# Experts' rows in 32-row units, up to four experts to a block, and inputs laid out by the host

## The chip, the core and the metric

The program runs on one core of a Trainium2 chip. TensorE (PE) multiplies, VectorE (DVE) and ScalarE (ACT) work on the results, GpSimd (POOL) issues the indirect transfers and SyncE (SP) most of the others. All numbers are fp32. The metric is the device time of one execution in microseconds (us); lower is better.

## What is computed

Two blocks of a network over 1024 tokens (and 256 context tokens), D = 1024 columns. The first has two layers, each with a modulation by a vector, a projection `h @ w_in`, latent attention, two convolution branches and an output projection. The second has three mixers (SSD, RWKV, GLA) and then a mixture of experts, the part that the change is mostly about:

```python
def _moe_ffn(h, router_w, router_b, w1, w3, w2, sw1, sw3, sw2):
    ...
    scores = jax.nn.sigmoid((h @ router_w).astype(f32))
    sel = scores + router_b.astype(f32)
    grp_score = lax.top_k(sel.reshape(t, N_GROUPS, per_group), 2)[0].sum(-1)
    _, top_g = lax.top_k(grp_score, TOPK_GROUPS)
    ...
    _, idx = lax.top_k(sel, TOP_K)
    wts = jnp.take_along_axis(scores, idx, axis=1)
    wts = wts / jnp.sum(wts, -1, keepdims=True) * ROUTED_SCALE
    ...
    def body(acc, blk):
        tok, wt, e = blk
        xb = h[tok]
        hid = jax.nn.silu(xb @ w1[e]) * (xb @ w3[e])
        return acc.at[tok].add(wt[:, None] * (hid @ w2[e]).astype(f32)), None
    ...
    shared = (jax.nn.silu(h @ sw1) * (h @ sw3)) @ sw2
    return routed.astype(h.dtype) + shared
```

Each of 1024 tokens goes to 8 of 64 experts, 8192 rows in all. An expert has w1 and w3 of 1024x256 and w2 of 256x1024, 3 MB together. The reference's own routing of these inputs gives the experts from 29 to 315 rows each.

## The kernel before

The kernel is one hand-ordered program: each stage is a set of functions, one for each engine, and an engine runs its instructions in the order in which they were emitted. Generators joined by `staged((n, lane), ...)` take turns, lane by lane, from step n on. Between stages `gate()` makes SP wait for everything and then lets all engines go on.

**Start.** `vectors()` (line 330) loads the constants and 34 small vectors as rows, turns them into columns on PE (line 348) and copies them out on DVE. `beginning()` then reads `x` and `ctx` in ten tiles of 128 tokens (`tokens`, line 456): SP loads a tile (line 470), PE turns it with eight 128x128 transposes (line 481), DVE copies it to `X` (line 489). Between the tiles run the modulation, whose matmuls (line 416) have two stationary columns and put four 512-column blocks of the weights into PSUM partitions 0, 32, 64 and 96, and the sums of squares of the norms (line 545, `n0` to `n2` for the token blocks of 256, 512 and 512). A norm ends with DVE lines 590 to 597 and ACT line 632, and then the projection (line 754) starts. `second_to_third` reads the two tiles of `ctx_2` in the same way.

**Routing** (`route_*` in `moe_sparse`, line 2680). After the choice of experts, PE counts each expert's rows (line 2767), DVE turns counts into blocks of 128 rows (lines 2851 to 2872), PE ranks the rows within each expert (lines 2770, 2773), and DVE works out a slot for each of the 8192 rows (`slots_of`). POOL writes token number and weight of each into the list `l_d` with 64 indirect DMAs (line 2947); SP then loads the list as `LB`, one column of 128 rows per block. Rows that no token has point at a dummy row.

**Expert blocks** (`blocks`, line 3046). NS = 96 blocks are always run and up to 127 where the counts want it (`rest`). The counts of these inputs fill 94. A block is 128 rows of one expert. SP loads the expert's three matrices into one of six slots (line 3072, three DMAs of 1 MB, only where a block is the first of its expert). POOL gathers the 128 rows of `h_d` (line 3082) three blocks ahead. For block q, in this order, PE does `up(q)`: eight matmuls with the turned rows as stationary operand and 512 columns of w1 and w3 moving (line 3128); `turn_h(q-1)`: two transposes (line 3136); `turn_x(q+1)`: eight transposes (line 3111); `down(q-1)`: four matmuls of 512 columns (line 3147). DVE and ACT empty PSUM after each (lines 3173 to 3220), and POOL adds the block's result to `r_d` by an indirect DMA (line 3090), which waits until the block before has landed. Each fp32 matmul is two instructions in the trace, so line 3128 has 16 for a block and line 3147 eight.

**End.** Eight tiles of 128 tokens are normalised and stored.

## Time and profile before

| | us |
|---|---|
| median of 3 runs | 5219.56 |
| lowest, highest | 5213.47, 5234.58 |
| the profiled execution | 5191.66 |
| its span, first to last instruction | 5189.8 |
| PE busy in it | 4463.7 (86%) |
| expert blocks, first matmul of line 3128 to last of line 3147 | 3996.57 to 5096.62 |
| DVE, ACT and POOL busy in the span | 2030.3, 1389.0, 516.4 |

The profile is one execution. Its rows name engine, line and operation, and what ended the idle time before them. A matmul's printed duration holds its way through the array, so neighbours overlap: the distance from one row's start to the next row's is the cost, not the sum of the durations.

### The profile page before, as it was taken

The page shows a single profiled execution, that of the slowest core. Times are in us where ns is not written, and L with a number is a line of the kernel's source. Part 1 is how long each engine was busy: PE and PEld are TensorE (multiplying, and loading weights), DVE is VectorE, ACT ScalarE, POOL GpSimd, SP SyncE. Part 2 cuts the span into 40 slices and gives each one's busy share as a digit, 9 for nine tenths or more (in the row PEclk, how much of TensorE's full clock was granted, in tenths as well). Part 3 has the DMA queues.
Part 4 walks back from the last instruction along what each step waited for, and adds up shares of the span by engine and source line. Part 5 has one row for each costly group of instructions (what it writes and reads, how often), then busy time and mean ns, then how long its engine had stood idle before and what let it go on. Part 6 is the DMA issues. An engine that isn't in the chain of part 4 may idle for free. (4 is left out here: it accounts for less than half of the span.)

```text
span 5189.8 us, 68095 instructions
## 1 busy us (share of the span) xinstructions
PE 4463.7 (86%) x25844; PEld 2575.7 (50%) x25844; DVE 2030.3 (39%) x4201; ACT 1389.0 (27%) x3178; POOL 516.4 (10%) x552
## 2 busy tenths in 40 slices
PE   5999799999987999999977437885977999999992
PEld 3454466644444664445466326773444444444441
DVE  2641556523416662320055576665252111111115
ACT  2111545411126551211133423331031111111110
POOL 0000000000000000000000002221005222222220
PEclk8999889999998999999977659886978999999996
DMA  4011000210110004302110110002015789899974
GB/s 179 18 60 60 13 13 17 91 63 28 58 59 5 13 15 189 114 30 72 62 44 2 60 36 3 3 3 71 36 56 193 215 245 320 276 283 317 305 236 126
DMA packets 290595, 517.79 MB, mean 100 GB/s; under 512 B 24853, under 2 KB 202847, under 8 KB 285023
## 3 DMA queue, kind: packets, MB, share of 16 engines
q1 hardware_dynamic: 249582, 377.69, 21.2%
q0 software_dynamic: 40688, 135.67, 9.3%
q8 instruction: 217, 3.56, 0.3%
q14 instruction: 108, 0.88, 0.1%
HBM read 511.88 MB, written 102.09 MB: 118 GB/s over the span
## 5 line engine op out<-in xcount | busy, mean ns | idle before, releaser
L754 PE MATMUL banks<-arena 128*128 128x512 f32 (+1 forms) x2928 | 1108.0, 540 | 15.4 <-DMA arena<-in_w_in 9.7
L754 PEld LDWEIGHTS banks<-arena 128*128 128x128 f32 x2928 | 558.9, 191 | 562.8 <-issue 522.7
L3128 PE MATMUL banks<-arena 128*128 x1536 | 678.0, 594 | 13.6 <-DMA arena<-in_exp_w 12.5
L3128 PEld LDWEIGHTS banks<-arena 128*128 128x128 f32 x1536 | 292.8, 191 | 382.5 <-issue 382.5
L941 PE MATMUL banks<-arena 128*128 128x512 f32 (+1 forms) x896 | 373.2, 571 | 25.2 <-DMA arena<-y_d 17.7
L1305 PE MATMUL banks<-arena 96*128 96x512 f32 (+1 forms) x800 | 377.0, 555 | 11.7 <-ACT arena L1408 10.0
L3147 PE MATMUL banks<-arena 128*128 x768 | 346.1, 593 | 1.4 <-ACT arena L3207 1.4
L1355 DVE TENSOR_REDUCE arena<-banks 128x1 f32<-128x512 f32 (+1 forms) x400 | 238.1, 595 | 243.2 <-PE banks L1305 241.6
L3186 DVE SCALAR_TENSOR_TENSOR arena<-arena,banks 128x256 f32<-128x256 f32 x96 | 46.2, 482 | 650.0 <-ACT arena L3220 650.0
L941 PEld LDWEIGHTS banks<-arena 128*128 128x128 f32 x896 | 171.9, 193 | 218.3 <-issue 212.5
L1313 PEld LDWEIGHTS banks<-arena 128*128 128x128 f32 x1312 | 171.9, 143 | 154.2 <-issue 123.5
L1408 ACT ACTIVATE arena<-banks,arena 128x512 f32<-128x512 f32 (+1 forms) x400 | 239.3, 606 | 16.1 <-DVE arena L1364 2.8
L3090 POOL DMA_INDIRECT r_d<-arena x96 | 151.7, 1580 | 824.0 <-DVE arena L3179 790.4
L1313 PE MATMUL banks<-arena 128*128 128x128 f32 x1312 | 214.0, 277 | 0.1
L1414 ACT ACTIVATE arena<-banks 128x256 f32<-128x256 f32 (+1 forms) x272 | 131.6, 484 | 289.4 <-PE banks L1313 289.2
L3147 PEld LDWEIGHTS banks<-arena 128*128 128x128 f32 x768 | 138.0, 189 | 139.7 <-issue 139.7
L1326 PE MATMUL banks<-arena 128*64 128x128 f32 x2624 | 191.9, 283 | 17.2 <-DVE arena L1369 13.1
L3220 ACT ACTIVATE arena<-banks 128x256 f32<-128x256 f32 x96 | 37.1, 387 | 618.8 <-PE banks L3128 618.8
L953 DVE SCALAR_TENSOR_TENSOR arena<-banks,arena 128x512 f32<-128x512 f32 (+1 forms) x56 | 39.9, 712 | 385.4 <-PE banks L941 385.4
L772 ACT ACTIVATE arena<-banks 128x512 f32<-128x512 f32 (+1 forms) x94 | 51.4, 547 | 514.1 <-PE banks L754 514.0
L780 ACT ACTIVATE arena<-banks 128x512 f32<-128x512 f32 (+3 forms) x95 | 50.5, 532 | 464.9 <-PE banks L754 459.5
L861 DVE SCALAR_TENSOR_TENSOR arena<-arena 128x1296 f32<-128x1296 f32 (+1 forms) x120 | 171.2, 1427 | 4.3
(500 smaller groups left out, 5859.2 us busy)
## 6 DMA issues: line engine op xcount, KB each, us to landing
arena<-in_exp_w SPq DMA_DIRECT2D x288, 1024.0 KB, 16.1
arena<-in_ada_w SPq DMA_DIRECT2D x12, 2048.0 KB, 7.4
arena<-in_w_in SPq DMA_DIRECT2D x19, 1024.0 KB, 5.7
arena<-in_w_mod SPq DMA_DIRECT2D x8, 2048.0 KB
arena<-in_w_in SPq DMA_DIRECT2D x7, 2048.0 KB
arena<-in_w_out SPq DMA_DIRECT2D x6, 2048.0 KB
arena<-in_w_mod SPq DMA_DIRECT2D x8, 1024.0 KB
u<-arena POOLq DMA_DIRECT2D x28, 256.0 KB, 2.3
```

Source lines behind the costliest of these rows:

```text
L754: i = e.matmul(self.out_of(n), lhs, rhs, start=k == 0, stop=k == KT - 1)
L861: e.scalar_tensor_tensor(z[:, lo:hi], a[:, lo - 15 + j:hi - 15 + j], reg(cw + 2 * j + ft, 1), z[:, lo:hi], ALU.mult, ALU.add).then_inc(Vn. ...
L941: i = e.matmul(bank(n % 4)[:, 0:nn], w[:, q, :], H[:, q, t0:t0 + nn], start=q == 0, stop=q == KT - 1)
L1305: op = e.matmul(bank(q)[:, 0:P * jn], QT[:, h, P * ti:P * ti + P], KTt[:, h, P * j0:P * (j0 + jn)], start=True, stop=True)
L1313: op = e.transpose(bank(3 + q)[:, P * j:P * j + P], pr[n % 2][:, P * (j0 + j):P * (j0 + j) + P], ident)
L1326: op = e.matmul(b[64 * (h % 2):64 * (h % 2) + 64, 0:P], V[:, j, 64 * h:64 * h + 64], ptr[n % 4][:, P * j:P * j + P], start=j == 0, stop=j ...
L1355: e.tensor_reduce(c[:, q:q + 1], bank(q)[:, 0:P * jn], AX.X, ALU.max).then_inc(Vn.hit(), 1)
L1408: e.activation(pr[n % 2][:, P * j0:P * (j0 + jn)], bank(q)[:, 0:P * jn], ACT.Exp, bias=c[:, 3:4], scale=SM, accum_out=c[:, 4 + q:5 + q]).t ...
L1414: e.activation(ptr[n % 4][:, P * j0:P * (j0 + jn)], bank(3 + q)[:, 0:P * jn], ACT.Copy).then_inc(Sn.hit("turn", n, q), 1)
L3090: e.indirect_dma_start(r_d, bass.IndirectOffsetOnAxis(ap=LB[:, q, 0:1].bitcast(U32), axis=0), og[(q - q0) % 2], None, compute_op=ALU.add). ...
L3128: op = e.matmul(ABK[(q - q0) % 2], xT[(q - q0) % 2][:, P * k:P * k + P], wv[:, k, :], start=k == 0, stop=k == KT - 1)
L3147: op = e.matmul(OBK[:, 512 * n:512 * n + 512], hT[(q - q0) % 2][:, P * f:P * f + P], w2[:, f, 512 * n:512 * n + 512], start=f == 0, stop=f ...
```

## The change

**Units of 32.** An expert's rows are padded to a multiple of 32 instead of 128. The experts are ranked by count. `CAPS` holds, for each rank, how many units of 32 rows it may have (316 units in all), and `TURN` the order of the ranks: the largest, the smallest, the second largest, the second smallest and so on. The units are laid in that order into 79 blocks of four units. Rows over an expert's cap go to `rest`, which runs only if there are any. By the reference's own routing of these inputs no expert is over its cap.

**Parts.** A block holds up to four experts. Its `parts` are runs of one, two or four units of one expert, at an aligned place: 32, 64 or 128 stationary columns, written to the PSUM partitions of those rows. For each slice k of `up`, and each quarter of `down`, PE does one matmul of 512 moving columns for each part. Worked out from `CAPS` and `TURN`: 37 blocks have one part of 128, 12 have two of 64, 4 have four of 32, and 26 have one of 64 and two of 32 (14 with the 64 first, 12 with it last). That is 155 parts in 79 blocks.

**Results.** A block's result is added to `r_d` in one DMA for each expert in it, 125 in all. The first piece of an expert waits until all pieces of the expert before have landed. There are three result buffers instead of two. The list is loaded four times, from row 0, 32, 64 and 96.

**Weights.** The host lays w1, w3 and w2 of an expert side by side, and SP loads 24 KB for each partition with one DMA per expert, into slot i % 6, once the expert six before it is done.

**Routing.** Ranks of the experts and their places are worked out on DVE with two more matmuls (`order`, `spots`) between `counts` and `ranks`.

**Start.** The host lays constants and vectors as one array of columns, and the tokens (and `ctx_2`) with the columns of D on the partitions. `vectors()`, its gate, the 96 transposes of tokens and their copies go. The norms start with the modulation, and a lane of them has two buffers of its own (`room_wide`).

```diff
+CAPS = [15, 12, 11] + [9] * 3 + [8] * 3 + [7] * 5 + [6] * 6 + [5] * 10 + [4] * 13 + [3] * 12 + [2] * 9
+TURN = [rank for pair in zip(range(32), range(63, 31, -1)) for rank in pair]
...
-    put("six", np.broadcast_to(6.0 * c[:, 1:11], (P, 10)))
+    room = np.array([CAPS[rank] for rank in TURN])
+    put("turn", np.stack([TURN, np.cumsum(room) - room, room], 1))
...
+def lay_tokens(a):
+
+    return a.T.reshape(KT, P, -1).transpose(1, 0, 2)
+
+
+def lay_experts(w1, w3, w2):
+
+    up = np.concatenate([w1, w3], 2).reshape(-1, KT, P, 512).transpose(0, 2, 1, 3).reshape(-1, P, 4096)
+    down = np.asarray(w2).reshape(-1, 2, P, D).transpose(0, 2, 1, 3).reshape(-1, P, 2048)
+    return np.concatenate([up, down], 2)
...
-    def vectors():
-        Tn, Vn, Sn, Gn = points("vectors")
-
-        def sync(e):
-            ld.turn(e)
-            e.dma_start(reg(CONST, CN), A["consts"]).then_inc(ld.hit("consts"), 16)
-            for i, pk in enumerate(packs):
-                for name, ap2 in pk:
-                    n, r = ap2.shape[0], cols[name] - V0 - 128 * i
-                    ld.turn(e)
-                    e.dma_start(ar[r:r + n, WORK + P * i:WORK + P * (i + 1)], ap2).then_inc(ld.hit("pack", name), 16)
...
-            for i in range(len(self.tiles)):
-                e.wait_ge(*ld.at(self.S, i))
-                if i >= nb:
-                    e.wait_ge(*Vn.at("copied", i - nb))
-                for k in range(KT):
-                    t = e.transpose(self.banks[i % nb][:, P * k:P * k + P], self.buf[i % 2][:, P * k:P * k + P], ident)
-                t.then_inc(Tn.hit("turned", i), 1)
...
+        def load(self, e):
+            for t0, n in self.blocks:
                 ld.turn(e)
-                e.dma_start(self.buf[i % 2], src).then_inc(ld.hit(self.S, i), 16)
-                yield
...
+    room_wide = lambda: Room([reg(o, 512) for o in (ST + 2048, ST + 2560, SPARE, SPARE + 512)], reg(ST + 3072, 512), None, [bank(4), bank(5)], per_lane=2)
...
-        NB, NR, NS, SLOTS = 127, NX + P, 96, 6
+        NS, NE, SLOTS = sum(CAPS) // 4, 50, 6
+        NB, NR = NS + NE, NX + 4 * P
...
-            ld.turn(e)
-            e.dma_start(LB, l_d.rearrange("(p b) c -> p b c", p=P)).then_inc(ld.hit("route", "list"), 16)
+            for row, rows, n in ((0, P, NB), (32, 96, NS), (64, 64, NS), (96, 32, NS)):
+                ld.turn(e)
+                e.dma_start(lists[row][0:rows], l_d.rearrange("(p b) c -> p b c", p=P)[row:row + rows, 0:n, :]).then_inc(ld.hit("route", "list", row), 16)
...
+            for ti in range(8):
+                op = e.matmul(bank(0)[0:64, 64:66], MK[:, 64 * ti:64 * ti + 64], ones[:, 0:2], start=ti == 0, stop=ti == 7)
             op.then_inc(Tn.hit("counts"), 1)
-            e.wait_ge(*Vn.at("count"))
+            e.wait_ge(*Vn.at("above"))
+            op = e.matmul(bank(0)[:, 128:192], ones[0:64, :], above[0:64, :], start=True, stop=True)
+            op.then_inc(Tn.hit("order"), 1)
+            e.wait_ge(*Vn.at("placed"))
+            op = e.matmul(bank(0)[:, 256:384], ones[0:64, :], placed[0:64, :], start=True, stop=True)
+            op.then_inc(Tn.hit("spots"), 1)
+            e.wait_ge(*Vn.at("spots"))
             op = e.matmul(bank(0), cm("lt"), MK, start=True, stop=False)
...
+            e.tensor_tensor(v8(over), v8(bank(0)), room.unsqueeze(1).broadcast_to([P, 8, 64]), ALU.is_ge).then_inc(Vn.hit(), 1)
+            e.tensor_tensor(v8(DST), v8(bank(0)), start.unsqueeze(1).broadcast_to([P, 8, 64]), ALU.add).then_inc(Vn.hit(), 1)
+            e.wait_ge(*Vn.own())
+            e.tensor_tensor(v8(over), v8(over), nbk.unsqueeze(1).broadcast_to([P, 8, 64]), ALU.mult).then_inc(Vn.hit(), 1)
+            e.wait_ge(*Vn.own())
+            e.tensor_tensor(DST, DST, over, ALU.add).then_inc(Vn.hit(), 1)
...
-        og = [al(1024) for _ in range(2)]
+        og = [al(1024) for _ in range(3)]
...
+                whose = [i for i, n in enumerate(turns) for _ in range(n)]
+                self.last = {i: q0 + n // 4 for n, i in enumerate(whose)}
+                self.parts = {}
+                for q in range(q0, self.q1):
+                    own, c, parts = whose[4 * (q - q0):4 * (q - q0) + 4], 0, []
+                    while c < 4:
+                        n = max(m for m in (1, 2, 4) if c % m == 0 and own[c:c + m] == [own[c]] * m)
+                        parts.append((own[c], slice(32 * c, 32 * (c + n))))
+                        c += n
+                    self.parts[q] = parts
...
-                for q in range(q0, self.q1):
-                    if q >= q0 + SLOTS:
-                        e.wait_ge(*Tn.at("down", q - SLOTS))
-                    v, first, s = self.word(e, q, 0, 63), self.word(e, q, 1, 1), self.word(e, q, 2, SLOTS - 1)
-                    slot = weights[:, bass.ds(s, 1), :]
-                    up = slot[:, :, 0:4096].rearrange("p a (k n) -> p (a k) n", k=KT)
-                    down = slot[:, :, 4096:6144].rearrange("p a (f n) -> p (a f) n", f=2)
-                    src = [A[n][0][bass.ds(v, 1)].rearrange("a (k p) n -> p (a k) n", p=P) for n in ("exp_w1_2", "exp_w3_2", "exp_w2_2")]
-                    for i, (dst, w) in enumerate(((up[:, :, 0:256], src[0]), (up[:, :, 256:512], src[1]), (down, src[2]))):
-                        ld.turn(e)
-                        e.dma_start(dst, w, cond=first).then_inc(ld.hit(S, "w", q, i), 16)
+                for i in range(self.n):
+                    if i >= SLOTS:
+                        e.wait_ge(*Tn.at("down", self.last[i - SLOTS]))
+                    v = e.value_load(er[0:1, 2 * i + self.j:2 * i + self.j + 1].bitcast(I32), min_val=0, max_val=63)
+                    ld.turn(e)
+                    e.dma_start(weights[:, i % SLOTS, :], A["experts"][bass.ds(v, 1)].rearrange("a p n -> p (a n)")).then_inc(ld.hit(S, "w", i), 16)
...
-                    if q > q0:
-                        e.wait_ge(*st.at(S, "r", q - 1))
-                    st.turn(e)
-                    e.indirect_dma_start(r_d, bass.IndirectOffsetOnAxis(ap=LB[:, q, 0:1].bitcast(U32), axis=0), og[(q - q0) % 2], None, compute_op=ALU.add).then_inc(st.hit(S, "r", q), 16)
+                    for n, (i, rows) in enumerate(self.rows[q]):
+                        if i and self.of[i][0] == (q, n):
+                            for before in self.of[i - 1]:
+                                e.wait_ge(*st.at(S, "r", *before))
+                        st.turn(e)
+                        e.indirect_dma_start(r_d, bass.IndirectOffsetOnAxis(ap=lists[rows.start][0:rows.stop - rows.start, q, 0:1].bitcast(U32), axis=0), og[(q - q0) % 3][rows, :], None, compute_op=ALU.add).then_inc(st.hit(S, "r", q, n), 16)
...
                     for k in range(KT):
-                        op = e.matmul(ABK[(q - q0) % 2], xT[(q - q0) % 2][:, P * k:P * k + P], wv[:, k, :], start=k == 0, stop=k == KT - 1)
+                        for i, rows in self.parts[q]:
+                            op = e.matmul(ABK[(q - q0) % 2][rows, :], xT[(q - q0) % 2][:, P * k:P * k + P][:, rows], weights[:, i % SLOTS, 512 * k:512 * k + 512], start=k == 0, stop=k == KT - 1)
                     op.then_inc(Tn.hit("up", q), 1)
...
-                            op = e.matmul(OBK[:, 512 * n:512 * n + 512], hT[(q - q0) % 2][:, P * f:P * f + P], w2[:, f, 512 * n:512 * n + 512], start=f == 0, stop=f == 1)
+                            for i, rows in self.parts[q]:
+                                o = 4096 + 1024 * f + 512 * n
+                                op = e.matmul(OBK[rows, 512 * n:512 * n + 512], hT[(q - q0) % 2][:, P * f:P * f + P][:, rows], weights[:, i % SLOTS, o:o + 512], start=f == 0, stop=f == 1)
...
-        most = blocks("blocks", 0, NS, (TC, VC, SC, GC), ld, st)
+        most = blocks("blocks", 0, [CAPS[rank] for rank in TURN], 0, (TC, VC, SC, GC), ld, st)
...
-        rest = blocks("rest", NS, NB, rest_counts, rld, rst)
-        more = lambda e: e.If(e.value_load(nt[0:1, :].bitcast(I32), min_val=0, max_val=NB) > NS)
+        rest = blocks("rest", NS, [4] * NE, 1, rest_counts, rld, rst)
+        more = lambda e: e.If(e.value_load(nt[0:1, :].bitcast(I32), min_val=0, max_val=NE) > 0)
...
-        first = first_into(0, False, "layer0mod", tok.there, lambda e, i: e.wait_ge(*TC.of("tokens").at("turned", NT - 1)))
+        tok = tokens("tokens", A["tokens"], TB3)
+        first = first_into(0, False, "layer0mod", tok.there, lambda e, i: None, room_wide())
         n0, n1, n2 = first.norms
-        staged((0, tok.sync(sp)), (2, mod.sync(sp)))
+        ld.turn(sp)
+        sp.dma_start(reg(V0, CN + A["columns"]), A["consts"]).then_inc(ld.hit("consts"), 16)
+        for e in (pe, dve, act):
+            e.wait_ge(*ld.at("consts"))
+        tok.load(sp), steps(mod.sync(sp))
         first.into.weight(sp, 0), first.sync(sp)
-        staged((0, tok.tensor(pe)), (2, mod.tensor(pe)), (2, n0.tensor(pe)), (10, n1.tensor(pe)), (18, n2.tensor(pe)), *first.lanes(pe, 20))
-        staged((0, tok.vector(dve)), (2, mod.vector(dve)), (2, n0.vector(dve)), (10, n1.vector(dve)), (18, n2.vector(dve)))
+        staged((0, mod.tensor(pe)), (0, n0.tensor(pe)), (2, n1.tensor(pe)), (10, n2.tensor(pe)), *first.lanes(pe, 12))
+        staged((0, mod.vector(dve)), (0, n0.vector(dve)), (2, n1.vector(dve)), (10, n2.vector(dve)))
         first.convolutions(dve), first.end.vector(dve)
-        staged((2, mod.scalar(act)), (2, n0.scalar(act)), (10, n1.scalar(act)), (18, n2.scalar(act)), *first.lanes(act, 20))
+        staged((0, mod.scalar(act)), (0, n0.scalar(act)), (2, n1.scalar(act)), (10, n2.scalar(act)), *first.lanes(act, 12))
         first.gpsimd(pool, "layer0mod", 4 * len(mod.groups) - 1)
 
     def first_to_second(ended):
 
         mod = modulation("layer1mod", A["w_mod"][1], "bmod1", "c", "cc", 3072, 32768, 3, mod_view(1, 24), first_columns(1))
         outp = out_project("layer0out", A["w_out"][0], TB3, mod_view(0, 24), ended.columns)
...
-    vectors()
-    gate()
     beginning()
```

Where the program stands on the engines that matter:

On PE, in the expert blocks (line 3128 before and 3102 now are `up`, 3136 and 3110 `turn_h`, 3111 and 3090 `turn_x`, 3147 and 3122 `down`; one row is one matmul of the source). Before, one block, with the register instruction that places each weight slot:

```order
L3128 ISA
L3128 MATMUL banks<-arena 128x512
L3136 MATMUL banks<-arena 128x128 x2
L3111 MATMUL banks<-arena 128x128 x8
L3147 ISA
L3147 MATMUL banks<-arena 128x512
```

Now, a full block, and the start of the next one (block 3, a part of 64 and two of 32):

```order
L3102 MATMUL banks<-arena 128x512 x8
L3110 MATMUL banks<-arena 128x128 x2
L3090 MATMUL banks<-arena 128x128 x8
L3122 MATMUL banks<-arena 128x512 x4
L3102 MATMUL banks<-arena 64x512
L3102 MATMUL banks<-arena 32x512 x2
L3102 MATMUL banks<-arena 64x512
L3102 MATMUL banks<-arena 32x512 x2
```

The order of the four steps is the same; a block of several parts alternates between widths at every slice. Each pair of the last rows is one of the eight slices that one row of 128x512 was.

On PE at the start of the program (line 416 before and 379 now is the modulation, 545 and 488 the sums of the norms, 481 the transposes of tokens). Before:

```order
L348 MATMUL banks<-arena 128x127
...
L481 MATMUL banks<-arena 128x128 x24
L416 MATMUL banks<-arena 2x512 x8
L481 MATMUL banks<-arena 128x128 x8
L416 MATMUL banks<-arena 2x512 x8
L545 MATMUL banks<-arena 128x256
L481 MATMUL banks<-arena 128x128 x8
```

Now:

```order
L379 MATMUL banks<-arena 2x512 x16
L488 MATMUL banks<-arena 128x256
L379 MATMUL banks<-arena 2x512 x8
L488 MATMUL banks<-arena 128x256
L379 MATMUL banks<-arena 2x512 x8
L488 MATMUL banks<-arena 128x256
L488 MATMUL banks<-arena 128x512
```

The transposes are gone and the 512-column sums of the second token block stand among the modulation's matmuls; before they came after it.

## Rows read from the trace of the kernel before

**Rows 1.** The page: the span, and busy time of each engine.

```profile
span 5189.8 us, 68095 instructions
...
PE 4463.7 (86%) x25844; PEld 2575.7 (50%) x25844; DVE 2030.3 (39%) x4201; ACT 1389.0 (27%) x3178; POOL 516.4 (10%) x552
```

**Rows 2.** Windows in the expert blocks: busy us of each engine, PEclk, DMA share, GB/s.

```profile
4025.00:5075.00 1050.00, 1050.00 (x3133) 516.54 (x3132) 171.74 (x276) 170.94 (x368) 233.98 (x182) 1.00 0.88 272
```

**Rows 3.** The timeline of PE over one block: start, us, line, count.

```profile
4704.12 7.03 PE L3128 MATMUL banks<-arena 128*128 x16
4710.98 0.38 PE L3136 MATMUL banks<-arena 128*128 128x128 f32 x2
4711.20 1.03 PE L3111 MATMUL banks<-arena 128*128 128x128 f32 x8
4712.08 3.60 PE L3147 MATMUL banks<-arena 128*128 x8
4715.52 7.03 PE L3128 MATMUL banks<-arena 128*128 x16
```

**Rows 4.** The DMA view, 3985 to 5085 us: queues, then issues to landing.

```profile
q1 hardware_dynamic: 150080, 200.88, 53.8%
q0 software_dynamic: 26935, 98.08, 34.0%
...
r_d<-arena POOLq DMA_INDIRECT x94, 9.4
```

**Rows 5.** The timeline of PE where the modulation stands between full matmuls.

```profile
2074.57 1.90 PE L416 MATMUL banks<-arena 128*2 128x512 f32 x16
2076.40 7.13 PE L941 MATMUL banks<-arena 128*128 128x512 f32 x16
2083.46 1.90 PE L416 MATMUL banks<-arena 128*2 128x512 f32 x16
```

**Rows 6.** The same where 32-column and 64-column matmuls (attention) stand.

```profile
307.62 1.02 PE L754 MATMUL banks<-arena 128*128 128x512 f32 x2
308.57 4.50 PE L748 MATMUL banks<-arena 128*32 128x256 f32 x48
...
706.83 0.38 PE L1313 MATMUL banks<-arena 128*128 128x128 f32 x2
707.15 1.31 PE L1326 MATMUL banks<-arena 128*64 128x128 f32 x20
708.29 0.39 PE L1331 MATMUL banks<-arena 128*64 128x128 f32 x4
708.61 1.12 PE L1305 MATMUL banks<-arena 96*128 96x512 f32 x2
```

**Rows 7.** The start: the timeline, and a window while the modulation's weights load.

```profile
69.51 1.88 PE L416 MATMUL banks<-arena 128*2 128x512 f32 x8
...
73.96 0.42 DVE L590 TENSOR_SCALAR arena<-banks 128x256 f32<-128x256 f32 x1
...
91.11 0.69 DVE L590 TENSOR_SCALAR arena<-banks 128x512 f32<-128x512 f32 x1 [11.69 <-PE banks L545]
...
104.85 5.15 PE L754 MATMUL banks<-arena 128*128 128x256 f32 x16
...
30.00:40.00 10.00, 7.69 (x50) 2.75 (x49) 1.76 (x2) 0.42 (x1) 0.00 (x0) 0.86 1.02 430
```

**Rows 8.** Windows from the first projection to the end of its stage.

```profile
105.00:145.00 40.00, 40.00 (x123) 24.09 (x122) 0.69 (x1) 6.60 (x12) 0.00 (x0) 0.96 0.00 0
145.00:506.00 361.00, 353.88 (x1015) 183.86 (x1013) 149.55 (x117) 58.50 (x93) 18.49 (x33) 0.99 0.13 42
```

**Rows 9.** The timeline of routing and of the first expert block.

```profile
3875.55 0.23 DVE L2851 COPY arena<-banks 128x64 f32<-128x64 f32 x1 [10.90 <-PE banks L2767]
3875.81 0.69 DVE L2853 TENSOR_TENSOR arena<-arena 128x512 f32<-128x512 f32 x1
3875.83 1.13 PE L2770 MATMUL banks<-arena 128*128 128x512 f32 x2 [0.32 <-DVE arena L2851]
...
3880.87 0.69 DVE L2875 TENSOR_TENSOR arena<-banks,arena 128x512 f32<-128x512 f32 x1
...
3984.13 0.60 ACT L3201 ACTIVATE arena<-banks 128x512 f32<-128x512 f32 x1 [20.12 <-PE banks L3111]
...
3996.57 10.09 PE L3128 MATMUL banks<-arena 128*128 x16 [12.54 <-DMA arena<-in_exp_w]
```

More of the change, by code:

```diff
@@ L3048, in moe_sparse, with __init__ @@
         class blocks:
-            def __init__(self, S, q0, q1, counts, ld, st):
-                self.S, self.q0, self.q1, self.ld, self.st = S, q0, q1, ld, st
+            def __init__(self, S, q0, turns, word, counts, ld, st):
+                self.S, self.q0, self.q1, self.ld, self.st = S, q0, q0 + sum(turns) // 4, ld, st
+                self.n, self.j = len(turns), word
                 self.points = lambda: [c.of(S) for c in counts]
-            def word(self, e, q, j, top):
-                return e.value_load(er[0:1, 3 * q + j:3 * q + j + 1].bitcast(I32), min_val=0, max_val=top)
+                whose = [i for i, n in enumerate(turns) for _ in range(n)]
[8 more added lines that the diff above has]
+                    self.parts[q] = parts
+                assert max(turns) <= 13 or turns[0] == max(turns) <= 16
+                self.rows = {q: [(i, slice(min(r.start for j, r in self.parts[q] if j == i), max(r.stop for j, r in self.parts[q] if j == i)))
+                                 for i in sorted({j for j, r in self.parts[q]})] for q in self.parts}
+                self.of = {i: [(q, n) for q in self.rows for n, piece in enumerate(self.rows[q]) if piece[0] == i] for i in range(self.n)}
@@ L3176, in down @@
                     e.wait_ge(*Tn.at("down", q))
-                    if q >= q0 + 2:
-                        e.wait_ge(*st.at(S, "r", q - 2))
-                    e.tensor_copy(og[(q - q0) % 2][:, 0:512], OBK[:, 0:512]).then_inc(Vn.hit("out", q), 1)
+                    if q >= q0 + 3:
+                        for n in range(len(self.rows[q - 3])):
+                            e.wait_ge(*st.at(S, "r", q - 3, n))
+                    e.tensor_copy(og[(q - q0) % 3][:, 0:512], OBK[:, 0:512]).then_inc(Vn.hit("out", q), 1)
                 turn_x(q0)
@@ L3210, in down @@
                     e.wait_ge(*Tn.at("down", q))
-                    if q >= q0 + 2:
-                        e.wait_ge(*st.at(S, "r", q - 2))
-                    e.activation(og[(q - q0) % 2][:, 512:1024], OBK[:, 512:1024], ACT.Copy).then_inc(Sn.hit("out", q), 1)
+                    if q >= q0 + 3:
+                        for n in range(len(self.rows[q - 3])):
+                            e.wait_ge(*st.at(S, "r", q - 3, n))
+                    e.activation(og[(q - q0) % 3][:, 512:1024], OBK[:, 512:1024], ACT.Copy).then_inc(Sn.hit("out", q), 1)
                 turn_x(q0)
@@ L3513, in make @@
         args[name] = nc.dram_tensor(f"in_{name}", a.shape, F32, kind="ExternalInput").ap()
-    a = host_constants()[0]
-    arrays["in_consts"] = a
-    args["consts"] = nc.dram_tensor("in_consts", a.shape, F32, kind="ExternalInput").ap()
+    args["column_at"], args["columns"] = host_columns({name: inputs[name].shape for _, name, _ in COLUMNS})
+    tokens = np.concatenate([inputs["ctx"][0], inputs["x"][0]], 0)
+    for name, a in (("consts", np.concatenate([lay_columns(inputs), host_constants()[0]], 1)), ("tokens", lay_tokens(tokens)),
+                    ("tokens_2", lay_tokens(inputs["ctx_2"][0])),
+                    ("experts", lay_experts(*(inputs[n][0] for n in ("exp_w1_2", "exp_w3_2", "exp_w2_2"))))):
+        a = np.ascontiguousarray(a, np.float32)
+        arrays[f"in_{name}"] = a
+        args[name] = nc.dram_tensor(f"in_{name}", a.shape, F32, kind="ExternalInput").ap()
     o = nc.dram_tensor("out_0", (1, NX, D), F32, kind="ExternalOutput").ap()
```

238 lines of the change are left out of this document (91 added, 147 removed).

## The prediction

> **What bounds the kernel now.** I read the page's busy times first [rows 1]: PE is busy 4463.7 of 5189.8 us, the others at most 39%. Then the windows: in the expert blocks PE is busy 1050 of 1050 us at the full granted clock [rows 2], so there PE's instructions are the time, and a change of a block's PE work comes through one to one. Then the timeline of one block [rows 3]: `up` of block q starts at 4704.12, of q+1 at 4715.52, so a block costs 11.40 us: 6.86 for the 16 instructions of `up` (0.429 each), 0.22 for `turn_h`, 0.88 for `turn_x`, 3.44 for the eight of `down`. 96 blocks at 11.4 are 1094 us, a fifth of the kernel. The DMA engines come close behind: 0.88 of their time [rows 2], of which 34.0% gathers and scatters and 53.8% weights [rows 4]. At the start PE waits for DMA, and is saturated after it [rows 8]; routing is a chain without PE [rows 9]. The measure of the sum is the profiled execution, 5191.7 us; the median of the runs shown lies 27.9 higher, and I add that at the end.
>
> **Fewer blocks.** 79 blocks run instead of 96: 17 × 11.40 = **−193.8 us**, if every block still cost 11.4. 37 blocks, of one part of 128, do: their instructions are the same. The other 42 have column tiles, and there it matters what the array runs together.
>
> **Tiles of one width.** The rows show this well. Line 748 has 32-column stationaries in four PSUM quarters: 48 instructions, of 256 and 512 moving columns, take 4.5 us [rows 6]; one after the other they would take 10 to 20. Line 416, with two columns in each quarter, takes 1.90 us for 16 instructions of 512 [rows 5], which one by one are 6.86. So four tiles of one width run together, a round of four every 0.429 us. Line 1326, 64 columns: 20 instructions of 128 columns in 1.14 us (707.15 to 708.29) [rows 6], half of the 2.1 to 2.2 that 20 times 0.107 make: two together. So the 12 blocks of two 64s and the 4 of four 32s stream at the pace of a full block.
>
> **The 26 mixed blocks.** This term decides. A slice there is 64, 32, 32, and the next slice 64 again. No place of the trace has 32 beside 64 columns, so it is bounded from both sides. From below: if the three parts run together as four 32s do, a slice costs the 0.86 us of its two instructions and nothing is added. From above: each change of width empties the array as all those shown do. Then the 64 streams alone (0.86), the two 32s together (0.86), and a slice pays two changes; 12 slices a block (8 of `up`, 4 of `down`). With 0.26 for two changes, between two of 0.11 (0.21, the one out of tiles and a like one back) and the 0.31 of [rows 5], which has an entry into full width that this one lacks: 12 × (0.86 + 0.26) = 13.4 us for a block, 26 × 13.4 = **+349 us**. At 0.21 it is 334. If the two halves of each fp32 matmul are issued in turns (first halves of all parts, then second halves, which the rounds of line 416 would fit too), a slice has four changes: 12 × (0.86 + 0.52) × 26 = 431. I take the upper case, 349, because it is the nearest row in kind: a change of width emptied the array wherever the trace has one (also between the 64s of line 1331 and the full-width matmul of line 1305, 0.32 us for four instructions of 128 columns, two rounds of 0.107 and a tenth [rows 6]), and the rows that show tiles together show tiles of one width only.
>
> The Trainium skill says this of the array: "TensorEngine Tiling (Array Packing)", Tiling Modes, Key Properties, has it that changing the tiling mode, not just the tile, drains TensorE. By that rule the sum is the one above, +349; it speaks against this change. The 0.31 us of rows 5 agrees with it for 128 and 32; no row shows 64 against 32.
>
> **Cover in the blocks.** DVE and ACT empty PSUM once a block as before (234 and 171 us of busy at most in 1050 [rows 2]): nothing. POOL issues 125 adds instead of 94, and the first of an expert waits for all of the expert before; an add lands 9.4 us after issue [rows 4]. 63 such steps of about 11.3 us are 712 us, below PE's 900 in the cheap case, and a block with up to four experts in it has up to four of them in a row (45 us) on three result buffers; averages of 0.8 per block fit, bursts may cost some us in the cheap case, none in the other, where a mixed block lasts 25. Weights: 64 × 3 MB as before; bandwidth is below with the cheap case.
>
> **Start.** Now the first norm's end, DVE line 590, comes at 73.96, 4.45 us after the last modulation matmul at 69.51, the second at 91.11, the first projection at 104.85 [rows 7]; from there PE is busy 100% and then 98% until 506 [rows 8], so a gain is kept. The transposes of tokens between them go. After: tokens 5.2 MB, vectors and constants 1.95 MB, and 12.6 MB of modulation weights, 19.8 MB, at 430 GB/s for 1.02 share, so 421 [rows 7]: 47 us, and the modulation ends at about 54 instead of 71. The squares of the second token block now stand ahead of its end, so that `n1` follows `n0` by its DVE chain (about 5.5 us) instead of 17, and the projection comes 14 later, as before: 76 to 78, **−27 us** (−18 if only the DMA gain counts, −32). What is late next is the weights of the projection, on the same queue. The 16 transposes of `ctx_2` go as well: **−2** (0 to −4; its 16 transposes are 1.8 us of PE by the 0.88 of `turn_x`'s eight).
>
> **Routing.** DVE's chain from the copied counts (3875.55) to the slots (3881.56, the end of line 2875) is 6.0 us [rows 9]; POOL's 64 writes come behind it and set the end. About 20 small DVE operations and two round trips through PE come in, each 0.2 to 0.7 us by these rows: **+8** (5 to 12). The first expert's weights now come as one DMA of 24 KB a partition; `up(0)` waits 12.5 us for them [rows 9], which larger packets may shorten: **−3** (−6 to 0).
>
> **Sum.** −193.8 + 20 + 349 − 27 − 2 + 8 − 3 = **+151**; 5191.7 + 151 = 5343, and on the runs' median 5219.6 + 151 = **5371 us**. With the mixed blocks at 334 or 431, and the rest at its ends, this case spans 5335 to 5475.
>
> **Rivals.**
> *Widths run together* (the other side). The place is the same 26 blocks: if the array takes 64 at one place and 32s at others without emptying, the +349 is nothing. It decides from about 6 us a mixed block: below that the change gains. For it: tiles of line 1326 and of 748 start within hundredths of a microsecond of each other, at their own places. Against it: every change in the trace costs its tenth. Then the blocks last 79 × 11.4 = 901 us, and DMA may bind: weights took 53.8% of 1100 us = 592, gathers and scatters 374, of which 79/96, 308, and the sum of 900 is what PE takes. Where the layout is densest in experts (a new expert for every block, some 28 blocks) a 3 MB load at 421 GB/s is 7.5 us and the block's transfers 3.9, as much as PE's 11.4; a stall of 0 to 20 us, 10 taken. −193.8 + 20 + 10 − 27 − 2 + 8 − 3 = −188: **5032 us** (5005 to 5050).
> A page of the Trainium skill would have it so: "TensorE: Matmul & The Clock Gate", Part 3, Packing small matmuls, says that each 32×32 tile of the array can hold other weights and work on another output slice, with starts about 4 ns apart. By it the price of a slice is the 0.86 and the sum is 5032; it does not speak of mixed widths.
> *Partly together*: the two changes are paid but the streams overlap at a boundary, some 6 to 8 us a mixed block, so within 26 us of no change: 5195 to 5245.
> *Parts never together*: 155 parts in series instead of 79, 76 × 12 × 0.86 = 784, less 194 and 24: about 5790. [Rows 5, 6] speak against it.
> *Overflow*: if the counts pass the caps, `rest` runs up to 50 blocks of 11.4, +570; the reference's counts leave none over.
>
> **How the numbers follow.** Changes of width empty the array: 0.72. Widths together: 0.22. Partly: 0.04. The last two: 0.02. The likeliest gives 5371, its own range 5335 to 5475. Two in ten may be left out, and the cheap case alone is more, so the range has to reach to it: 5005 to 5475. About 0.5% is what a measurement of this kernel can tell from no change, 5193.5 to 5245.7. Faster 0.22, same 0.04, slower 0.74.
>
> **What would show it.** In the timeline of PE, a mixed block: `up` of about 16 us (24 matmuls of the source, 48 instructions) against 6.86, period near 25; if it is near 7, the rival holds. A full block stays at 11.40, one of four 32s near 11.7 to 12. The span from first `up` to last `down`: about 1270 us against 920 to 930. The first projection at 76 to 78; the slots 14 us after the counts; a first weights wait near 9. PE waiting for DMA of weights, or `up` for a gather behind POOL's chain, in the middle of the blocks would make the terms for cover wrong; a price for a width change above 0.16 or four changes a slice would put the time over 5400.

## The result, and the profile after

| | before | after |
|---|---|---|
| median, us | 5217.33 | 5390.17 |
| lowest, highest | 5213.47, 5234.58 | 5378.20, 5392.14 |

The ratio is 1.032, with a 95% interval of 1.0292 to 1.0348: slower. The forecast was 5371 and slower. Beside the others in a later job the changed kernel took 1.0285 (1.0261 to 1.0309) of the kernel before.

The page of the changed kernel, for [rows 1], has a longer span and more PE time:

```profile
span 5376.3 us, 67000 instructions
...
PE 4617.0 (86%) x27010; PEld 2429.1 (45%) x27010; DVE 1984.1 (37%) x4148; ACT 1363.1 (25%) x3110; POOL 521.9 (10%) x564
```

The window over its blocks, for [rows 2] (busy us and instructions of PE, PEld, DVE, ACT, POOL, then PEclk, DMA share, GB/s): PE is still the whole of the time, at full granted clock, and the DMA engines have more room than before, 0.68 instead of 0.88.

```profile
4016.00:5280.00 1264.00, 1261.89 (x4501) 407.20 (x4500) 146.15 (x235) 149.51 (x314) 254.74 (x199) 1.00 0.68 221
```

The timeline of PE in its blocks, for [rows 3] (start, duration, line, count; 3102 is `up`, 3110 `turn_h`, 3090 `turn_x`, 3122 `down`): first a full block's `up`, then two mixed ones.

```profile
4038.17 7.03 PE L3102 MATMUL banks<-arena 128*128 128x512 f32 x16
4045.04 0.38 PE L3110 MATMUL banks<-arena 128*128 128x128 f32 x2
4045.26 1.04 PE L3090 MATMUL banks<-arena 128*128 128x128 f32 x8
4046.13 3.60 PE L3122 MATMUL banks<-arena 128*128 128x512 f32 x8
4049.66 15.95 PE L3102 MATMUL banks<-arena 128*64 128x512 f32 x48
...
4070.22 15.95 PE L3102 MATMUL banks<-arena 128*32 128x512 f32 x48
...
4087.35 8.01 PE L3122 MATMUL banks<-arena 128*64 128x512 f32 x24
4095.29 4.99 PE L3102 MATMUL banks<-arena 128*128 128x512 f32 x11
```

A full `up` takes 6.87 from start to start (4038.17 to 4045.04), as before. A mixed one takes 15.88 to the next step, 1.985 a slice, and a mixed `down` 7.94 against 3.43. A mixed block is thus 9.0 + 4.5 = 13.5 us dearer than a full one.

The weight loads of the first mixed `up` (PEld, the loads of stationary operands) show the order within its slices:

```profile
4049.66 0.19 PEld L3102 LDWEIGHTS banks<-arena 128*64 128x64 f32 x2 [0.76 <-issue]
4050.66 0.14 PEld L3102 LDWEIGHTS banks<-arena 128*32 128x32 f32 x4 [0.81 <-issue]
4051.64 0.19 PEld L3102 LDWEIGHTS banks<-arena 128*64 128x64 f32 x2 [0.84 <-issue]
```

Both halves of the 64 come first, then both halves of the two 32s. The 64 takes 1.00 us (4049.66 to 4050.66) and the pair of 32s 0.98 (to 4051.64), where two rounds are 0.86. So there are two changes of width in a slice and not four, each of 0.12 to 0.14, and the 64 and the 32s work one after the other.

The text ahead has up to four experts to a block, but no block has four. Worked out from `CAPS` and `TURN`, 37 blocks have one expert, 38 have two and 4 have three. A mixed block has two: three units of one (a part of 64 and one of 32) and one unit of the other.

The start, for [rows 7], on PE and DVE (379 is the modulation, 386 its columns, 488 the sums of the norms, 697 the projection):

```profile
60.43 1.56 PE L488 MATMUL banks<-arena 128*128 128x256 f32 x4
62.00 0.66 PE L386 MATMUL banks<-arena 128*128 128x128 f32 x4
62.49 1.02 PE L488 MATMUL banks<-arena 128*128 128x512 f32 x2
70.87 3.78 PE L488 MATMUL banks<-arena 128*128 128x512 f32 x4 [7.36 <-ACT arena L551]
84.87 2.08 PE L488 MATMUL banks<-arena 128*128 128x512 f32 x2 [10.21 <-ACT arena L551]
86.73 4.55 PE L697 MATMUL banks<-arena 128*128 128x256 f32 x16
```

The first projection stands 18.1 us earlier than in [rows 7] (86.73 against 104.85).

Set side by side by stages, the pair of profiles has a surprise. From the counts (line 2713 now, 2767 before) to the first `up` it is 170.9 us now and 123.0 before, 48 more where the sum had 5. These are lines of ACT and POOL of the changed kernel in that stretch:

```profile
3921.41 1.03 ACT L2971 ACTIVATE arena<-banks 128x1024 f32<-128x1024 f32 x1 [7.46 <-remote]
3956.41 0.39 ACT L2979 ACTIVATE arena<-banks 128x256 f32<-128x256 f32 x1 [33.97 <-remote]
...
3950.16 0.97 POOL L2914 DMA_INDIRECT l_d<-arena  x1 [0.30 <-issue]
```

Line 2979 empties an `up` of the shared expert which PE had finished at 3917.5. ACT stands still for 34 us, until some 5 us after POOL's last write of the list, and names no engine of the program as its releaser. The profile of before has no such wait. The experiments had two questions, then: what the mixed blocks cost, and whose these 45 us are.

### The profile page after: what moved, and what is told of

It reads as the page before. It is cut to its first block and busy times, and to the rows that moved or that the text cites. A ratio compares the mean times of both kernels' runs of the same rounds, so it can differ in the third digit from the quotient of the medians.

```text
span 5376.3 us, 67000 instructions
## 1 busy us (share of the span) xinstructions
PE 4617.0 (86%) x27010; PEld 2429.1 (45%) x27010; DVE 1984.1 (37%) x4148; ACT 1363.1 (25%) x3110; POOL 521.9 (10%) x564
## 5 line engine op out<-in xcount | busy, mean ns | idle before, releaser
L697 PEld LDWEIGHTS banks<-arena 128*128 128x128 f32 x2928 | 558.3, 191 | 562.6 <-issue 522.5
L3102 PE MATMUL banks<-arena 128*32 128x512 f32 (+2 forms) x2480 | 798.4, 603 | 3.2 <-DMA arena<-in_experts 2.4
L3102 PEld LDWEIGHTS banks<-arena 128*32 128x32 f32 (+2 forms) x2480 | 218.9, 137 | 565.5 <-issue 562.7
L3122 PE MATMUL banks<-arena 128*32 128x512 f32 (+2 forms) x1240 | 400.1, 602 | 1.3 <-ACT arena L3180 1.3
L3069 POOL DMA_INDIRECT r_d<-arena x125 | 181.4, 1451 | 980.6 <-DVE arena L3152 456.9
L884 PEld LDWEIGHTS banks<-arena 128*128 128x128 f32 x896 | 172.7, 194 | 218.9 <-issue 213.0
L1256 PEld LDWEIGHTS banks<-arena 128*128 128x128 f32 x1312 | 171.3, 143 | 153.0 <-issue 122.2
L3122 PEld LDWEIGHTS banks<-arena 128*32 128x32 f32 (+2 forms) x1240 | 104.7, 137 | 239.7 <-issue 238.0
L3152 DVE COPY arena<-banks 128x512 f32<-128x512 f32 x79 | 54.7, 693 | 338.6 <-PE banks L3122 338.6
```

Source lines behind the costliest of these rows:

```text
L697: i = e.matmul(self.out_of(n), lhs, rhs, start=k == 0, stop=k == KT - 1)
L884: i = e.matmul(bank(n % 4)[:, 0:nn], w[:, q, :], H[:, q, t0:t0 + nn], start=q == 0, stop=q == KT - 1)
L1256: op = e.transpose(bank(3 + q)[:, P * j:P * j + P], pr[n % 2][:, P * (j0 + j):P * (j0 + j) + P], ident)
L3069: e.indirect_dma_start(r_d, bass.IndirectOffsetOnAxis(ap=lists[rows.start][0:rows.stop - rows.start, q, 0:1].bitcast(U32), axis=0), og[(q ...
L3102: op = e.matmul(ABK[(q - q0) % 2][rows, :], xT[(q - q0) % 2][:, P * k:P * k + P][:, rows], weights[:, i % SLOTS, 512 * k:512 * k + 512], s ...
L3122: op = e.matmul(OBK[rows, 512 * n:512 * n + 512], hT[(q - q0) % 2][:, P * f:P * f + P][:, rows], weights[:, i % SLOTS, o:o + 512], start=f ...
```

## The experiments

### All parts of a mixed block 32 wide

```diff
+                    if len({r.stop - r.start for i, r in parts}) > 1:
+                        parts = [(i, slice(c, c + 32)) for i, r in parts for c in range(r.start, r.stop, 32)]
                     self.parts[q] = parts
```

> The changed kernel with one edit: in the 26 mixed blocks the part of 64 is issued as two parts of 32, so that every block has parts of one width. Theory (each change of width empties the array and the two widths never stream together): a mixed block falls from 24.9 us in the changed kernel's trace to 11.4 plus about 0.3 for its pair of changes, 26 x 13.3 = 345 us less than the changed kernel, about 5040 in all; up of such a block is 6.9 to 7.1 us instead of 15.9. Rival (a mixed block is dear for having several experts: weight waits, adds in a row): no change, about 5390. Second question: with blocks at 11.4 the transfers may bind, which would show as PE waiting for weights or gathers in the dense middle, 0 to 30 us.

Measured: 5046.66 us, 0.9723 (0.9707 to 0.974) of the kernel before, which took 5189.84 in that job. In the later job, with the same kernel beside others:

> The all-32 kernel beside the two-sum kernel on one chip: 0.972 of the kernel before, as before; with or without the wait in the routing as the others of this job.

5061.72 us, 0.9753 (0.9736 to 0.9769). Its PE timeline shows the mixed block with four parts (64 instructions instead of 48), then its `down`:

```profile
4019.28 7.07 PE L3104 MATMUL banks<-arena 128*32 128x512 f32 x64
4026.28 0.44 PE L3112 MATMUL banks<-arena 128*128 128x128 f32 x2
4026.55 1.04 PE L3092 MATMUL banks<-arena 128*128 128x128 f32 x8
4027.52 3.64 PE L3124 MATMUL banks<-arena 128*32 128x512 f32 x32
```

More instructions in less than half the time: `up` is 7.00 from start to start instead of 15.88. The experts in the block, their weights, gathers and adds are the same. So it is the mixture of widths that was dear, and the rival that blames the number of experts falls. The forecast of 5040 was met, but with a remainder. The blocks lasted 992 us (3972.74 to 4964.4, in the later job) where the sum says 921, and PE waited, nine times, for gathers. The waits of PE and POOL in this kernel (us in total, times, longest):

```profile
PE banks L3092 <- DMA arena<-h_d,arena: 45.4, 9, 6.4
...
POOL r_d L3071 <- DMA r_d<-arena: 293.5, 32, 21.9
```

In the changed kernel the same chain of adds stood behind the slower blocks: its PE waited for no gather there.

### Mixed widths, changed once a step

```diff
-                    for k in range(KT):
-                        for i, rows in self.parts[q]:
+                    widths = sorted({r.stop - r.start for i, r in self.parts[q]})
+                    for width in widths:
+                      for k in range(KT):
+                        for i, rows in [p for p in self.parts[q] if p[1].stop - p[1].start == width]:
```

and `down` likewise.

> The changed kernel with its parts (64 beside 32s) kept, but a mixed block goes through all eight slices of up with its 32s first and then through all eight with its 64 (down likewise), so that widths change once a step instead of twice a slice. Theory by sizes: of the 13.5 us extra of a mixed block 12 x 0.86 = 10.3 is the second stream and stays, and 3.1 is the changes, of which all but about 0.5 goes: a mixed block at about 22.3 instead of 24.9, 26 x 2.6 = 68 us less, about 5320. If the changes are free and the extra is something else: no change. If streams of the two widths overlap when they are long: far more than 68.

Measured: 5275.86 us, 1.0162 (1.0144 to 1.0181). Its PE timeline:

```profile
4013.82 14.07 PE L3104 MATMUL banks<-arena 128*32 128x512 f32 x48
4027.83 0.44 PE L3112 MATMUL banks<-arena 128*128 128x128 f32 x2
...
4047.75 7.20 PE L3126 MATMUL banks<-arena 128*32 128x512 f32 x24
4054.88 7.13 PE L3104 MATMUL banks<-arena 128*128 128x512 f32 x16
```

`up` is 14.01 instead of 15.88, `down` 7.13 instead of 7.94: 2.68 less a block, 70 for the 26, against 68 expected. The stage shrank by 58 (1264.2 to 1206.3) and the time by 60 against the changed kernel's 5336 in a job where the kernel before took the same. Of the other 12 us, 5.0 are one wait of PE for a gather, which the changed kernel had not; the rest was not searched for. The split is clear all the same. Of the 15 changes inside an `up` 14 are gone and of the 7 inside a `down` 6: 2.68 / 20 = 0.13 for each. What is left of the 14.01 is two streams of 6.87 and little else. This order can't show whether the widths would overlap, because an engine runs its instructions in the order of the program, and there the two widths are neighbours at one place of a step only; that they do not is shown by the changed kernel's own order, where they are neighbours all the time and a slice still holds 0.86 twice. Of a mixed block's 13.5 us about 10.3 are the second stream and 3 the changes of width. From the changed kernel's slice, 1.985 - 1.717 = 0.27 for two changes.

### Full blocks only

```diff
-CAPS = [15, 12, 11] + [9] * 3 + [8] * 3 + [7] * 5 + [6] * 6 + [5] * 10 + [4] * 13 + [3] * 12 + [2] * 9
+CAPS = [16, 12, 12] + [12] * 3 + [8] * 3 + [8] * 5 + [8] * 6 + [8] * 10 + [4] * 13 + [4] * 12 + [4] * 9
```

> The changed kernel with each cap rounded up to a multiple of four units: 404 units, 101 full blocks, no tiles anywhere; ranks, layout, host-laid weights and the new start stay. Additive theory: 5 more blocks than the kernel before x 11.4 = +57, start about -27, the routing's measured excess of about +40: between 5230 and 5300. It shows the parts of the change apart from packing. If laying weights by the host also shortens blocks, less; PE is at its stream rate, so none is expected.

Measured: 5226.66 us, 1.0072 (1.0053 to 1.0091), 37 us more than the kernel before in that job, just under the span that was expected, because the routing had no stall here. The window over its 101 blocks:

```profile
3973.00:5130.00 1157.00, 1152.50 (x3426) 565.84 (x3426) 187.90 (x302) 187.44 (x403) 254.48 (x197) 1.00 0.81 262
```

1152.5 / 101 = 11.41 a block. So ranks, layout and the weights in one DMA leave a full block as it was, and a block is worth its 11.4.

### The start alone

Routing, blocks and experts' weights as before, with the new constants, vectors, tokens and beginning.

> The kernel before with the new start alone: constants, vectors and tokens (and ctx_2) laid by the host, no transposes of tokens, norms with the modulation; routing and expert blocks as before. Theory from the trace of the changed kernel: first projection 19 us earlier (85.9 against 104.9), kept to the end by PE's saturation, and some 2 to 10 us more by the second stage: 20 to 30 us less than the kernel before, ratio 0.994 to 0.996. Rival: the gain is lost at a later gate or in a wait for DMA: ratio 0.998 to 1.000.

Measured: 5210.55 us beside 5233.76, 0.996 (0.9941 to 0.998): 23 us less, with the first projection at 86.98 (the 85.9 of the expectation was a weight load; the projection's first matmul was at 86.73). The interval only touches the rival's 0.998. But this kernel, which has the routing of the kernel before to the letter, had ACT's stall too:

```profile
3908.94 1.02 ACT L2948 ACTIVATE arena<-banks 128x1024 f32<-128x1024 f32 x1 [5.08 <-remote]
3939.80 0.39 ACT L2956 ACTIVATE arena<-banks 128x256 f32<-128x256 f32 x1 [29.84 <-issue]
3945.41 0.39 ACT L2962 ACTIVATE arena<-banks 128x256 f32<-128x256 f32 x1 [5.22 <-remote]
```

### Whose is the stall

The changed kernel without any edit, in the job of the start alone:

> The changed kernel itself, unedited, beside the others on one chip. In its profile ACT stood still for 34 us in the routing (3922 to 3956) with no releaser of its own program, and the first up came 46 us later, counted from the choice of experts, than in the three variants, whose routing code is the same. If that wait belongs to this program as built, it is there again and the time is 1.030 to 1.035 of the kernel before; if it was that execution's alone, the routing from the counts (first matmul of the counts to the first up) takes 126 us as in the variants instead of 171, and the ratio falls to about 1.024.

5383.79 us, 1.0285. The stall was there again (142.2 us from the first rank matmul to the first spread matmul), so my first reading was that it belongs to this program. The three variants had 91.1, though, and they differ only in blocks or caps. What differed was the job. So the next job held both kernels:

> The kernel before itself, profiled beside the others of this job. In four profiles of two chips (the changed kernel twice, the start alone, two sums) ACT stood still in the routing until some 5 us after GpSimd's last write of the list, 45 to 50 us in all; in those of a third chip (all-32, grouped, full units), and in the first profile of the kernel before, it did not. Theory: that wait belongs to the chip or to how the programs are loaded, not to the change: all profiles of this job show it or none, this one too (from the first rank matmul to the first spread matmul 87 us without it, 130 to 140 with it). Rival: it belongs to the changed start or routing: here 87 us whatever the others show.

> The changed kernel again beside the kernel before of the same job. If the wait of ACT in the routing goes with the chip, it is here exactly if it is in the profile of the kernel before, and the two spans differ by 140 us (blocks +165, start -19 to -29, routing +8 to 10, end +2, and a few us elsewhere), not by the 186 of the first pair of profiles. If it goes with the changed program: there in this one alone, and the spans differ by 186.

The kernel before took 5181.12 and the changed one 5336.07 in their one run each. None of the four profiles of this job has the stall: from rank to spread 85.5 us in the kernel before, 91.2 in the changed one. The line of ACT that had stood for 34 us waits for 5.8 at most now (us in total, times, longest), behind an ordinary matmul:

```profile
ACT arena L2979 <- PE banks L2941: 40.7, 7, 5.8
```

The same program as built has the stall in two jobs and not in a third: it goes with the job (the chip, or where things were loaded), not with the change. All three profiles of one job had it, all three of another and all four of this one had not. The kernel before fits: 5179 to 5198 in the two jobs whose profiles are free of it, 5213 to 5245 in the others, though it was never itself profiled with it. What holds ACT there is open. It ends about when POOL's 64 indirect writes do: ACT's last long wait of that kind ended 4 to 6 us behind the last write in three of the four profiles, and with its issue in that of the start alone. No experiment took the writes away.

This gives a clean pair. Its two spans differ by 154.9 us, not by the 186 of the first pair and not by the 140 that was expected without the stall:

| | before | after | difference |
|---|---|---|---|
| first projection | 103.72 | 86.77 | -17.0 |
| counts | 3864.27 | 3847.77 | -16.5 |
| first `up` | 3988.08 | 3973.87 | -14.2 |
| last `down` ends | 5087.63 | 5238.03 | +150.4 |
| span | 5179.3 | 5334.2 | +154.9 |

The expectation of 140 had a start of -19 to -29 and a few us more saved between the stages, which are not there. The end of the blocks, on PE, in either (5083.94 + 3.69 and 5234.33 + 3.70):

```profile
5083.94 3.69 PE L3147 MATMUL banks<-arena 128*128 x8 [0.83 <-ACT arena L3207]
```

```profile
5234.33 3.70 PE L3122 MATMUL banks<-arena 128*128 128x512 f32 x8 [0.74 <-ACT arena L3180]
```

### Two arrays of results

The remainder of the first experiment was to go by letting an add pass the one before. Experts of odd place add to a second array, which starts at zero and is added in the end stage.

```diff
-                        if i and self.of[i][0] == (q, n):
-                            for before in self.of[i - 1]:
+                        if i > 1 and self.of[i][0] == (q, n):
+                            for before in self.of[i - 2]:
...
-                        e.indirect_dma_start(r_d, ...
+                        e.indirect_dma_start((r_d, r2_d)[i % 2], ...
...
+                e.wait_ge(*ld.at("end", "r2", i))
+                e.tensor_tensor(r, r, rq[i % 3], ALU.add).then_inc(Vn.hit(), 1)
```

> The changed kernel with mixed blocks all in 32s (as in the first experiment) and two result arrays in DRAM: experts of even place add to one, those of odd place to the other, so that the first add of an expert waits for the expert two before instead of one before; the end stage loads and adds the second array. Theory (in the all-32 kernel PE's 40 us of waits for gathers come from POOL, which stands before an add until the expert before has landed, with the next gather queued behind it): those waits and the clock lost after them go, 40 to 55 us less in the blocks; the end pays about 8 to 12 us for 4 MB more of loads and eight more additions. Net 30 to 45 us less than the all-32 kernel, about 0.965 of the kernel before. Rival (the DMA engines' share of 0.88 sets those waits): the waits stay, now behind no add, and the time is 5 to 12 us more than all-32.

Measured: 5061.42 us, 0.9666 (0.964 to 0.9692), in a job with the stall, so it could not be set beside the first experiment. Hence once more, beside it:

> The two-sum kernel beside the all-32 kernel: by their traces its blocks take 924 instead of 980 us and its end 107 instead of 97, so it should be 46 us under all-32 on the same chip, 0.963 to 0.966 of the kernel before. Rival (the earlier difference of the traces was one of chips): within 10 us of all-32.

5008.30 against 5061.72 us: 53 less, more than the 30 to 45 and the 46 that were expected; 0.9649 (0.9633 to 0.9665) of the kernel before. The windows over the blocks, of the all-32 kernel and of this one:

```profile
3973.00:4964.00 991.00, 943.51 (x5126) 385.61 (x5126) 146.23 (x235) 148.76 (x314) 254.80 (x199) 0.97 0.85 282
```

```profile
3976.00:4900.00 924.00, 921.78 (x5126) 378.25 (x5126) 146.22 (x235) 148.85 (x314) 254.76 (x199) 1.00 0.89 303
```

The DMA engines are busier (0.89) and no longer waited for. POOL waits for 97.8 us of adds instead of 293.5, and PE's waits for gathers are gone. With them goes what PE lost beside them: the same 5126 instructions took 943.5 us at a mean granted clock of 0.97, and 921.8 at 1.00. The 45 of waits and the 22 of clock are the 67 us by which the blocks are shorter; 10 more in the end stage and 3 more before the blocks leave the 53. 79 blocks of 11.40 and 20 for the entries make 921, which is what is left. This version beats both kernels by more than their uncertainty.

## Why the prediction was right

**The sign and the size** were right: 5390 against 5371, and 154.9 against +151 in the clean pair, by the mechanism that was given 0.72. That the sum is met to 4 us is in part luck: the terms of the tiles were 9 too dear, the start 10 too hopeful and the end stage, +4.5, not in it.

- *Fewer blocks, -193.8*: right. The full blocks kept their 11.40, and 101 full blocks gave 11.41 each.
- *Tiles of one width run together, +20 for entries*: right. With all parts of one width, PE was busy for 921.78 us in 79 blocks, 21.2 over 79 x 11.40; the 101 full blocks were 1.1 over theirs. That leaves 20.1 for the 42 tiled blocks, 0.48 each.
- *Mixed blocks, +349*: right. The slice was forecast at 0.86 + 0.86 + 0.26 and measured 1.985. By the same count the changed kernel's 1261.89 us hold 360 for the 42 tiled blocks, where the sum had 349 + 20 = 369. With 0.48 for each of the 16 others, 352 are left for the mixed ones, 13.6 each with their entries. A mixed block has 22 changes inside its steps, where the sum took 24 and the entries besides; at 0.13 that is 7 of the 9 too much. Of the Trainium skill's two pages, the rule of "TensorEngine Tiling (Array Packing)", Tiling Modes, that a change of mode drains TensorE, held for 64 and 32 as well: each change cost its 0.12 to 0.14 us. That the tiles work side by side, as "TensorE: Matmul & The Clock Gate", Part 3, says, held for tiles of one width only: in the changed kernel's slice the 64 takes 1.00 us and the two 32s 0.98, one after the other.
- *Start, -27*: too large, and past its own smallest of -18; -17.0 at the first projection (23 less in time for the start alone as a kernel). The step that failed is the end of the modulation at 54, taken from the bytes. It came at 62: from 48.71 PE itself set the pace, a group of eight instructions of line 379 and four of line 488 each 3.3 us, 1.48 of it the sums of the norms that had been moved in between. And the second norm's line 533 came 9.9 after the first (72.98 and 63.06), not 5.5.
- *Routing, +8*: the slots stood 14.1 us after the counts' copy, where 14 was said; POOL's first write 22.1 behind the counts' first matmul instead of 13.0, so +9.1.
- *First weights, -3*: larger. `up(0)` waited 13.2 us for them in the kernel before and 2.3 now. Of these 11 not all are won: from POOL's last write to the first `up` it is 20.0 instead of 26.3, so -6. From the counts to the first `up` that makes 126.1 instead of 123.8 (the clean pair).
- *ctx_2, -2*: not to be told from the 1 to 10 us by which stages between 900 and 3800 us differ from one profile to another.
- *Not in the sum*: the end stage, +4.5; its cause was not looked for.
- *The cheap case* was sized as 5032 with 10 us for transfers. The all-32 kernel, which has its times on PE, took 0.9723 and 0.9753, so 5073 and 5089 of the first job's 5217. The 10 us are the term that was too small, and for the wrong reason. I had put down POOL's chain of adds at 712 us for the whole stage and called it shorter than PE's 900. It is, in the mean; but POOL stood up to 21.9 us before one add, and the gather queued behind it was late nine times, 67 us with the clock. No block has the four experts that the prediction feared, only 4 have three, and 38 have two. That the rival would have gained holds.

## What to carry to other kernels

A packing into narrower tiles gains only while everything between two full-width steps has one width: price each change of width (here 0.13 us) and, above all, count the streams that then stand one behind the other. Issue the wide part as several narrow ones at the width of its neighbours, which costs instructions but hardly any time (7.00 us for an `up` instead of 6.87). Where an in-order queue holds both the loads ahead and the stores behind, look at the longest wait in it, not at the mean of its chain.

## What the runs showed of the hardware

- Two widths of column tiles, 64 and 32, at different places of the array and of PSUM, did not stream at once with the 64 before the 32s or behind them: 26 blocks of about 25 us against 11.7 to 11.8 with four 32s. Other orders, such as the 64 between the 32s, were not tried.
- Four parts of 32, three of them with the same moving data, stream almost as fast as one part of 128: 7.00 us for 64 instructions, 6.87 for 16.
- ACT stood still beside GpSimd's indirect writes, for 34 us at a stretch in one profile and in two or three shorter stretches in others, in every profile of two jobs and in none of two others, with the same program on both sides. From the first rank matmul to the first spread matmul a kernel took 133 to 142 us with the stall and 85 to 91 without. A pair of profiles from different jobs was wrong by 32 us of its 186, and by 46 in the routing; the pair from one job was not.
